# Down products of the last two experts by column halves, and another order at the start of the second layer, in a two-layer diffusion trunk step

## The reference, cut to what matters

```python
def _expert_choice_ffn(h, w_router, w_gate, w_up, w_down):
    ...
    xg = jax.vmap(lambda hb, ib: hb[ib])(h, idx)
    hid = jax.nn.silu(jnp.einsum('becd,edf->becf', xg, w_gate)) * jnp.einsum('becd,edf->becf', xg, w_up)
    out = jnp.einsum('becf,efd->becd', hid, w_down) * g[..., None].astype(h.dtype)
    return jax.vmap(lambda ob, ib: jnp.zeros((n, d), ob.dtype).at[ib.reshape(-1)].add(ob.reshape(-1, d)))(out, idx)

for l in range(DEPTH):
    ...
    h = _rmsnorm(xl, norm_mix[l]) * (1.0 + ml[1]) + ml[0]
    aq, ak, av, bq, bk, bv, cq, ck, cv, cg, gates = _split_projection(h, w_in[l])
    ...
    xl = xl + ml[5] * _expert_choice_ffn(h, w_router[l], w_exp_gate[l], w_exp_up[l], w_exp_down[l])
```

## Time and profile before

| | before |
|---|---|
| median of three runs | 1913.78 us (1913.78 to 1914.08) |
| profiled execution | 1913.8 us |
| its span | 1913.8 us, 21853 instructions |
| PE busy | 1790.3 us (94%) |
| DVE, ACT, POOL busy | 612.9, 382.9, 273.9 us |
| moved by DMA | 553.16 MB, mean 289 GB/s |
| granted TensorE clock | 0.998 of full speed, mean |

### The profile page before, as it was taken

How to read it: one execution, slowest core, us unless ns; L and a number is a source line. 1 busy time by engine, 2 the same in 40 slices (tenths; PEclk the granted TensorE clock), 3 DMA queues, 4 the chain that set the end, 5 groups by cost and what they waited for, 6 DMA issues and landing times.

```text
span 1913.8 us, 21853 instructions
## 1 busy us (share of the span) xinstructions
PE 1790.3 (94%) x9074; PEld 1027.3 (54%) x9074; DVE 612.9 (32%) x1296; ACT 382.9 (20%) x861; POOL 273.9 (14%) x153
## 2 busy tenths in 40 slices
PE   6999999999999988788799999999999998888887
PEld 3565556999734333233265555689995343333323
DVE  2632343565411211111155333445643111111103
ACT  3223334101301010010132242240112110101002
POOL 0200005953100000000002000266610000000000
PEclk9999999999999999999999999999999999999999
DMA  9525152424899999999992244214359999999996
GB/s 386 193 91 205 64 212 108 163 102 197 343 424 427 428 428 428 427 428 428 402 388 99 88 182 175 101 45 177 132 220 393 429 427 426 428 427 428 427 428 258
DMA packets 54851, 553.16 MB, mean 289 GB/s; under 512 B 5984, under 2 KB 9952, under 8 KB 13280
## 3 DMA queue, kind: packets, MB, share of 16 engines
q1 hardware_dynamic: 50976, 549.13, 69.2%
q10 hardware_dynamic: 3776, 2.62, 0.4%
HBM read 547.54 MB, written 4.19 MB: 288 GB/s over the span
## 4 chain that ended last, share of the span: by engine, by line
PE 68%; DMA 29%; DVE 1%; issue 1%; ACT 0%; SPq 0%; DVEq 0%; ACTq 0%
PE psum L1266 17%; PE psum L1493 14%; PE psum L1057 12%; DMA ring<-in_w_up 8%; DMA dense<-in_w_down 8%; DMA ring<-in_w_gate 8%; PE psum L1059 7%; DMA dense<-in_w_gate 4%; PE psum L454 2%; PE psum L1018 2%; PE psum L1185 2%; PE psum L1105 1%; PE psum L1463 1%; PE psum L1361 1%; PE psum L1039 1%; PE psum L1144 1%
## 5 line engine op out<-in xcount | busy, mean ns | idle before, releaser
L1493 PE MATMUL psum<-ring,dense 128*64 128x512 f32 x960 | 216.8, 596 | 34.0 <-DMA ring<-in_w_gate 20.1
L1057 PE MATMUL psum<-hT,ring 128*128 128x384 f32 x720 | 238.8, 488 | 0.0
L1057 PEld LDWEIGHTS psum<-hT,ring 128*128 128x128 f32 x720 | 135.0, 190 | 90.7 <-issue 1.4
L1493 PE MATMUL psum<-dense 128*64 128x512 f32 x704 | 158.6, 595 | 22.1 <-DMA dense<-in_w_gate 15.1
L1493 PEld LDWEIGHTS psum<-ring,dense 128*64 128x64 f32 x960 | 68.5, 137 | 173.6 <-issue 139.4
L2312 DVE TENSOR_TENSOR state<-state,psum 128x512 f32<-128x512 f32 x32 | 22.0, 688 | 371.2 <-PE psum L1493 333.2
L830 POOL TENSOR_TENSOR tmp<-square 128x384 f32<-128x384 f32 x5 | 5.0, 999 | 859.5 <-ACT square L1625 859.5
L1059 PE MATMUL psum<-ring,hT 128*128 128x512 f32 x288 | 126.5, 594 | 0.0
L1923 ACT ACTIVATE kcT<-psum 32x512 f32<-32x512 f32 x60 | 35.2, 587 | 426.1 <-PE psum L1493 425.7
L1493 PEld LDWEIGHTS psum<-dense 128*64 128x64 f32 x704 | 49.1, 137 | 127.5 <-issue 93.2
L2349 DVE COPY decays<-psum 16x512 f32<-16x512 f32 x60 | 41.3, 689 | 222.5 <-PE psum L1493 222.1
(11 more groups left out here) (304 smaller groups left out, 2514.2 us busy)
## 6 DMA issues: line engine op xcount, KB each, us to landing
dense<-in_w_gate SPq DMA_DIRECT2D x34, 2048.0 KB, 36.1
ring<-in_w_in SPq DMA_DIRECT2D x60, 1024.0 KB, 9.5
ring<-in_w_up SPq DMA_DIRECT2D x30, 2048.0 KB, 38.9
ring<-in_w_gate SPq DMA_DIRECT2D x30, 2048.0 KB, 36.2
wide<-in_w_up SPq DMA_DIRECT2D x22, 2048.0 KB, 37.6
dense<-in_w_down SPq DMA_DIRECT2D x20, 2048.0 KB, 40.3
ring<-in_w_mod SPq DMA_DIRECT2D x38, 1024.0 KB, 9.4
ring<-in_w_down SPq DMA_DIRECT2D x18, 2048.0 KB, 40.2
```

Of the source, the lines that this page charges most:

```text
L1057: last = M.matmul(psum[:, bank, 0:T], ring[:, n % RING, k, cols], hT[:, k, :], start=k == 0, stop=k == KD - 1)
L1493: last = M.matmul(psum[HALF * half:HALF * (half + 1), bank, :], lhsT(k), SPARE_BLOCKS[2 * kk + half] if spare else w[:, kk, half * SLAB:(h ...
```

## The change

It does six things.

1. Expert 14's down weights are stored by column halves too, as expert 15's. The four last parts run as (14, 0), (15, 0), (14, 1), (15, 1) (`LAST_PARTS`), each into a half bank of its own, and are loaded in that order. Expert 15's transposes come before all four.
2. Chunks 0 to 3 of the last scatter, their residual and the squares of chunks 0 to 2 come before part (15, 1); the rest comes behind it.
3. Places 91 to 93 are loaded as two transfers of 1 MB, place 94 as 1 MB and two of 0.5 MB.
4. Second layer: the slabs are loaded as mod 1, first half of w_in 0, mod 3, second half of w_in 0. PE runs mod 1, the first halves of groups 0 and 1, mod 3, both transposes, and the first halves of groups 2 and 3 (`BEGUN` 4, was 2).
5. The first two names of `FREED_LAST` are exchanged, so that ring slot 0 of the second layer is freed by place 86 and slot 3 by place 93.
6. To match, the three places loaded behind the modulation slabs are issued as 5, 4, 3 and no longer 3, 4, 5 (`CHAIN_AT`).

```diff
-BEGUN = (4, 2)
+BEGUN = (4, 4)
...
-        LAST_BANKS = [S[1], TR[0]]
+        def last_psum(expert, part):
+            return psum[:, {NE - 2: (TR[1], S[0]), NE - 1: (S[1], TR[0])}[expert][part], 0:SLAB // 2]
...
+        LAST_PARTS = [(NE - 2, 0), (NE - 1, 0), (NE - 2, 1), (NE - 1, 1)]
...
-            if FILL[f] in (("z", 0, 2), ("z", 0, 3)):
+            if FILL[f] in [("z", l, g) for l in range(DEPTH) for g in (2, 3)]:
                 return O[FILL[f][2] - 2]
...
-        FIRST_SLABS = [..., [("mod", 1), ("mod", 3), ("w_in", 0)]]
+        FIRST_SLABS = [..., [("mod", 1), ("w_in", 0), ("mod", 3)]]
-        FREED_LAST = [("w_in", 14), ("branch", 2), ("w_out", 0), ("w_out", 1)]
+        FREED_LAST = [("branch", 2), ("w_in", 14), ("w_out", 0), ("w_out", 1)]
-        CHAIN_AT = [3, 4, 5, 6, 7, 8]
+        CHAIN_AT = [5, 4, 3]
...
+                        sp.dma_start(to[:, 0:4], of[:, 0:4]).then_inc(expert_in[i % EXPERT_BUFFERS], 16)
+                        if i + 1 < len(IN_PLACES):
+                            sp.dma_start(to[:, 4:KD], of[:, 4:KD]).then_inc(last_rest[i - FIRST_LAST], 16)
+                        else:
+                            sp.dma_start(to[:, 4:6], of[:, 4:6]).then_inc(last_rest[i - FIRST_LAST], 16)
+                            sp.dma_start(to[:, 6:KD], of[:, 6:KD]).then_inc(last_end, 16)
...
                         norm_sum(TR[0], 0)
-                        fill(START_FILL[layer][0:2])
+                        fill(START_FILL[layer][0:1])
                         z_first_half(0)
-                        fill(START_FILL[layer][2:4])
                         z_first_half(1)
+                        fill(START_FILL[layer][1:4])
+                        z_first_half(2)
+                        z_first_half(3)
...
+                    def last_down_part(n):
+                        expert, part = LAST_PARTS[n]
+                        i = FIRST_LAST + n
+                        w = whole_slab(BUFFERS[layer][i % EXPERT_BUFFERS])
+                        rows = hidT if expert == NE - 2 else last_hidT
+                        pe.wait_ge(expert_in[i % EXPERT_BUFFERS], expert_landed(layer, i))
+                        for k in range(KD):
+                            if k == KD // 2:
+                                pe.wait_ge(last_rest[n], at(last_rest[n], 16))
+                            if k == 6 and n + 1 == len(LAST_PARTS):
+                                pe.wait_ge(last_end, at(last_end, 16))
+                            for side in range(2):
+                                last = M.matmul(last_psum(expert, part)[...], rows[:, k % 4, k // 4, :], w[...], start=k == 0, stop=k == KD - 1)
+                        last.then_inc(down_full, 1)
...
-                    last_down_product()
-                    scatter(QUADS - 1)
+                    hidden_transposed(NE - 1)
+                    pe.wait_ge(down_act, at(down_act, NE - 2))
+                    pe.wait_ge(down_dve, at(down_dve, NE - 2))
+                    last_down_part(0)
+                    pe.wait_ge(ht_read, at(ht_read, NE))
+                    last_down_part(1)
+                    last_down_part(2)
+                    scatter(QUADS - 1, range(4))
+                    last_down_part(3)
+                    scatter(QUADS - 1, range(4, KD))
...
+                        if n + 1 == len(LAST_PARTS):
+                            squares(layer + 1, 0, range(3))
...
+                        if n + 1 == len(LAST_PARTS):
+                            residual(QUADS - 1, range(4))
```

More of the change, by code:

```diff
@@ L722, in load_last @@
                     def load_last(i):
-                        part = i - (len(IN_PLACES) - 2)
-                        for half in range(2):
-                            rows = slice(half * KD // 2, (half + 1) * KD // 2)
-                            signal = (expert_in[i % EXPERT_BUFFERS], last_rest[part])[half]
-                            sp.dma_start(whole_slab(BUFFERS[layer][i % EXPERT_BUFFERS])[:, rows], whole_slab(w_down[layer, NE - 1, part])[:, rows]).then_inc(signal, 16)
+                        e, part = LAST_PARTS[i - FIRST_LAST]
+                        to, of = whole_slab(BUFFERS[layer][i % EXPERT_BUFFERS]), whole_slab(w_down[layer, e, part])
+                        sp.dma_start(to[:, 0:4], of[:, 0:4]).then_inc(expert_in[i % EXPERT_BUFFERS], 16)
[4 more added lines that the diff above has]
+                            sp.dma_start(to[:, 6:KD], of[:, 6:KD]).then_inc(last_end, 16)
                     EARLY = 3
@@ L777, in _ @@
                             sp.wait_ge(signal, count)
-                        load_slab(layer, n)
+                        if layer and SLABS[layer][n] == ("w_in", 0):
+                            load_half(layer, n, 0)
+                        else:
+                            load_slab(layer, n)
+                        if layer and n + 1 == after_first:
+                            load_half(layer, SLABS[layer].index(("w_in", 0)), 1)
                     for c, (l, j) in enumerate(CHAIN[layer]):
@@ L1469, in gather, with product @@
                             last.then_inc(xg_full, 1)
-                    def product(expert, s0, bank, signal, lhsT, between=None):
+                    def product(expert, s0, bank, signal, lhsT):
                         for s in (s0, s0 + 1):
-                            if between and s > s0:
-                                between()
                             spare = EXPERT_ORDER[SPARE] == (expert, s)
@@ L1527, in down_product @@
                             pe.wait_ge(down_dve, at(down_dve, expert))
-                        product(expert, 4, TR[1], down_full, lambda k: hidT[:, k % 4, k // 4, :],
-                                (lambda: hidden_transposed(NE - 1)) if expert == NE - 2 else None)
-                    def last_down_product():
-                        pe.wait_ge(ht_read, at(ht_read, NE))
-                        for part in range(2):
-                            i = IN_PLACES.index(LAST_DOWN[part])
-                            w = whole_slab(BUFFERS[layer][i % EXPERT_BUFFERS])
-                            pe.wait_ge(expert_in[i % EXPERT_BUFFERS], expert_landed(layer, i))
-                            for k in range(KD):
-                                if k == KD // 2:
-                                    pe.wait_ge(last_rest[part], at(last_rest[part], 16))
-                                for side in range(2):
-                                    last = M.matmul(psum[HALF * side:HALF * (side + 1), LAST_BANKS[part], 0:SLAB // 2], last_hidT[:, k % 4, k // 4, :],
-                                                    w[:, k, side * SLAB // 2:(side + 1) * SLAB // 2], start=k == 0, stop=k == KD - 1)
-                            last.then_inc(down_full, 1)
@@ new lines, in down_product @@
+                        product(expert, 4, TR[1], down_full, lambda k: hidT[:, k % 4, k // 4, :])
+                    def last_down_part(n):
[10 more added lines that the diff above has]
+                            for side in range(2):
+                                last = M.matmul(last_psum(expert, part)[HALF * side:HALF * (side + 1)], rows[:, k % 4, k // 4, :],
+                                                w[:, k, side * SLAB // 2:(side + 1) * SLAB // 2], start=k == 0, stop=k == KD - 1)
+                        last.then_inc(down_full, 1)
@@ L1552, in picks_transposed, with scatter @@
                         last.then_inc(pgT_full, 1)
-                    def scatter(quad):
+                    def scatter(quad, chunks=range(KD)):
                         pe.wait_ge(down_act, at(down_act, QUAD * (quad + 1)))
@@ L1608, in copy_first, with squares @@
                     A_.activation(to, psum[:, pair_banks(kind, u)[0], 0:TOKENS], ACT.Copy).then_inc(pair_copied[kind], 1)
-                def squares(layer, mixer):
+                def squares(layer, mixer, chunks=range(KD)):
                     at = from_layer(layer)
                     first = mixer * KD
-                    for k in range(KD):
+                    for k in chunks:
                         if mixer and k == 5:
@@ L2312, in gated, with residual @@
                         V.tensor_tensor(hid, act, psum[:, S[1], :], ALU.mult).then_inc(hid_ready, 1)
-                    def residual(quad):
-                        for n in range(KD):
+                    def residual(quad, chunks=range(KD)):
+                        for n in chunks:
                             dve.wait_ge(sc_full, at(sc_full, KD * quad + n + 1))
@@ L2324, in _ @@
                     gated(0)
-                    for e in range(NE):
+                    for e in range(NE - 1):
                         quad, nth = divmod(e, QUAD)
```

88 lines of the change are left out of this document (43 added, 45 removed).

## The result

Over 20 runs each the changed kernel takes 1916.59 us (1914.86 to 1918.23) against 1914.05 (1913.23 to 1915.43): 1.0013 times the time before, 95% interval 1.0007 to 1.0018. A second set (11 runs beside 26 of before) gave 1916.46 against 1914.13, 1.0014 (1.0005 to 1.0023). The two differences are +2.5 and +2.3 us, **+2.4**: no change by the 0.2% bound, as predicted, but the time is 0.2 us above the predicted range and the difference 1 us more than the forecast's +1.4. One run of 8364 us (of the kernel before) and one of 3771 us (of experiment 7) stand far apart from all others and are left out everywhere.

A forecast was written before the change was run, and what follows sets the result against it. PE was taken to bound some stages and weight loads others. Both tails -0.6 us and the second layer's start +2.0 made +1.4 on 1913.8, so 1915.2 us, with 1912.8 to 1916.4 expected 8 times in 10.

The forecast's parts named there:

- The last wait for a DMA: Each layer's tail: PE last waits for (14, 1)'s second half, near 951.4 and 1890.3 us; (15, 1) runs without waiting.
- The work behind it: Each layer's tail: from (14, 1)'s landing to the sixth chunk PE needs 9.94 us instead of 5.26, 4.68 more.
- the copy that nothing of PE's covers any more, 0.86 and some 0.05 of hand-over: Tail, between part (15, 1) and the fifth chunk: PE waits for that part's copy, 0.86 us plus some 0.05.
- How much earlier (14, 1) lands: Each layer's tail: the last awaited landing comes 5.1 us earlier in the first layer, 4.9 in the second.
- The half microsecond a layer that the text kept for hand-overs: Allowance in the bounds (-1.6 to +0.4 us) around the tails' -0.6, for hand-overs that the trace lacks in this order.
- The start: Start of the second layer: one modulation product first, PE at ACT's pace +1.7 us, transposes waiting +0.3, together +2.0.
- The start costs nothing: Rival, second layer's start: slack in later waits between scores and softmax gives the 2.0 us back, 1913.2 us; 22%.
- Half of the scatter leaves the path: Rival, both tails: only a quarter part, one copy and the fifth chunk remain, -3.1 us a layer, 1907.6 or 1909.6; 4%.
- Place 3 comes late: Rival, first experts: expert 1's first gate slab, behind two slabs, comes late; 8 us late would give 1919 us; 3%.
- the rival with a fixed price: Rival, last four slabs' loads: three more transfers a layer at 2.4 us each, +14 us, 1929.6 us; 1%.
- The baseline: Starting time of the sum: the kernel before at 1913.8 us, profiled execution and span taken as equal, median 1913.78.

The follow-up runs named there:

- experiment 7: The changed kernel with both modulation products again ahead of the first half group, its load order and four groups begun ahead kept: 1914.16 us against 1914.11 before.
- experiment 3: The changed kernel with chunk 3 of the last scatter moved behind the last part (15, 1): 1915.24 us against 1914.31 for the kernel before.
- experiment 2: The kernel before with only the new end of each layer's experts, the second layer's start as before: 1915.08 us against 1914.31.
- experiment 1: The kernel before with only the new start of the second layer, the end of each layer's experts as before: 1916.16 us against 1914.31.
- experiment 4: The kernel before with chunks 0 and 1 behind (15, 0), 2 behind (14, 1), others behind (15, 1), nine loads: 1912.91 us against 1914.31.

## Why the prediction was wrong, step by step

**The last wait for a DMA: right.** It is the second half of (14, 1), at 951.29 (forecast 951.4). In the second layer it is 1891.8 where 1890.3 was forecast, 1.5 us later, because this layer's experts begin later (by the mean of place 90 1.75 us). Part (15, 1) starts at 955.98 (956.0) and runs its 32 matmuls without a wait, so the finer split of its load bought nothing.

**The work behind it: mis-sized by 0.33 us a layer.** The text had 9.94 us from the landing to the sixth chunk, 4.68 more than before. It is 961.55 - 951.29 = 10.26, and to the norm sum 12.27 - 7.26 = 5.01 more. The failing term is "the copy that nothing of PE's covers any more, 0.86 and some 0.05 of hand-over". From the start of (15, 1) to the fifth chunk it is 4.84 us and not 4.58: PE's end to DVE's start is 0.06, and DVE's end (959.71 + 0.86 = 960.57) to PE's start at 960.82 is another 0.25. So the term was 0.26 short: the text priced one hand-over where there are two, and the second isn't small. Behind DVE's end PE's queue still shows two rows of waits, at 960.61 (L1582) and 960.72 (L1584), and then the weight load of the fifth chunk, at 960.79. In experiment 3, where the queue is down to its last wait when the copy ends, PE starts 0.10 us behind DVE (959.84 to 959.94). The difference, 0.15 us a layer, fits the three waits with which each call of `scatter` begins: the edit calls it anew right at this chunk. That is read from the order of the rows; no run took these waits out alone. The other 0.1 is between the chunks and part (15, 1). Experiment 3 takes nearly all of this wait out (0.16 us is left) and gains 0.81 us a layer, so it was on the path.

**How much earlier (14, 1) lands: mis-sized by 0.2 us.** The text took 5.1 and 4.9 us; by the means it is 19.79 - 15.01 = 4.78, and 4.79 in the second layer. In before's own trace the same two places are 5.03 and 5.02 us apart by their means (14.76 and 14.82 behind place 90's). The rest, 0.25 and 0.23, is (14, 1) landing later behind finer loads, which the text said cost nothing beyond their bytes: with six loads the same piece is at 14.76 and 14.90. The second layer's 4.9 was nearer only because the lag fell from 3.27 to 3.12 us between the two landings that it was read from. Together: -0.6 forecast for both tails, 2 x (5.01 - 4.78) = **+0.5** by the traces, and +0.8, +0.05 and +0.6 in the three pairs that differ by this tail (experiment 2, experiment 7, which keeps the new load order as well, and the changed kernel against experiment 1). The error is 1.1 us. The half microsecond a layer that the text kept for hand-overs would have held the 0.33, but not the landings' 0.2 on top of it.

**The start: right, +2.0 forecast.** From norm sum to full groups it is 983.92 - 963.52 = 20.40 us, less 5.16 for the two half groups that now lie ahead, so 15.24 against 976.70 - 963.67 = 13.03: **+2.2**. Its parts: PE idle 1.13 behind the one product (forecast "about 1"), the pair of half groups paced by ACT (5.80 against 5.33 for the pair that follows), and the transposes 1.44 against 1.04, 0.4 where 0.3 was forecast. The sum of means is 2 x 0.23 + 2.2 = +2.7, and +2.4 to +2.5 is measured. Experiments 1 and 7 do and undo it, +1.9 and -2.4.

**The rivals.** "The start costs nothing" falls with experiments 1 and 7. "Half of the scatter leaves the path" falls: PE had to do 4.7 us of work behind (14, 1) before it could begin (15, 1), as the text said. "Place 3 comes late" would show as a wait in the first experts, and the rival with a fixed price as 2.4 us for each further load. In the first layer the first expert's row is 0.27 us later than before (524.91 against 524.64) and place 90's mean landing 0.13 (933.99 against 933.85), so nothing is lost between them, and a load costs 0.075.

**The baseline.** The text took the profiled execution's time to be its span, 1913.8. It was some 1.8 more. The forecast rests on the median as well, so this moved nothing, but with it the trace would have been known to be a late one, with long lags in it. The median itself has moved, though: 1913.78 is that of three runs, and over 20 it is 1914.05. Of the 1.4 us between the forecast 1915.2 and 1916.59, 0.3 are the baseline and 1.1 the two tails. As a difference to before the range was -1.0 to +2.6, and +2.5 lies just inside it: that the time falls outside the range is the baseline's doing, that it comes so near its edge is the tail's.

## What to carry to other kernels

Work that is moved ahead of the last weights is worth only what it leaves behind it: keep enough of it behind the last product to cover that product's copy and both hand-overs (0.06 us to the copy, 0.10 back, or 0.25 with more waits left on PE's queue), and move the rest. The same holds for each product that work is moved behind (1.01 us in experiment 4). Don't take away the filler under which other engines build an operand (1.8 us of product here) to start the operand's consumer sooner: it starts at the other engines' pace. When a wait for a DMA is priced from one trace, take the mean over the engines and the lag apart, and look at what the next stage's weights allow before more of the tail is cut.

## What was not expected of the hardware

**The lag of the slowest engine.** Means of the 16 landings repeat to 0.03 us over 383 us, and the last of the 16 comes 1.4 to 3.5 us behind their mean, differently in each run and layer. It is large enough for the 0.6 to 1.1 us of standard deviation between runs, though only profiled executions show it and no run varied it. It is small again once the queue has run empty: the kernel before issues the second layer's first slabs from 953.6 us on, when the first of the engines has been done since 951.4, and they land 0.3 us behind their mean; the changed kernel issues them from 932.7, into a full queue, and they land 2.2 us behind. The Trainium skill ("DMA: Bandwidth & Descriptors", section "Why a DMA increments its semaphore by 16 and not by 1") says that the engines finish independently and that only the full count means that the data has landed; the traces agree, with this size.

**Issuing a load can take 4.2 us.** SyncE's own rows in the changed kernel, from the part loads to the next layer's first slabs:

```profile
911.23 4.24 SPq L735 DMA_DIRECT2D ring<-in_w_down  x1
915.51 4.24 SPq L737 DMA_DIRECT2D ring<-in_w_down  x1
...
924.08 4.24 SPq L739 DMA_DIRECT2D dense<-in_w_down  x1
...
932.66 6.72 SPq L692 DMA_DIRECT2D ring<-in_w_mod  x2
```

Before, (14, 1)'s two loads were issued at 911.0 and 911.3; now its second comes at 915.5. It still lands in its turn, 35.74 us later and not 40.0, so the delay costs nothing while the queue is full. A cause that fits is a queue that takes a new load only when an old one has drained, but no run here varied its depth.
